# Gate table of an expert layer: GpSimd builds the gated one-hots alone, and 22 expert units are multiplied in split form

## The chip, the core and the metric

The kernel runs on one core of a Trainium2 chip. Its engines are called as the profile calls them: PE (TensorE, the matrix engine; PEld is its weight load), DVE (VectorE), ACT (ScalarE), POOL (GpSimd), and SP, whose queue starts the DMAs. The metric is the device time of one launch in microseconds. Before the change it is 2589.73 us, the median of 3 runs (2589.39 to 2591.72).

## The reference

Two layers of a transformer-like block and then a second block of another kind; the change touches the feed-forward part of each of the two layers, a "PEER" layer with 16384 experts, of which every token picks 16 for each of 8 heads. Everything is float32.

```python
q = (ht @ w_q).reshape(n_tok, PEER_HEADS, PEER_QDIM)       # 256 tokens, 8 heads
v1, i1 = lax.top_k(s1, PEER_TOPK)                          # 16 best of 128 first keys
v2, i2 = lax.top_k(s2, PEER_TOPK)                          # 16 best of 128 second keys
cand = (v1[..., :, None] + v2[..., None, :])...            # 256 pairs
top, pos = lax.top_k(cand, PEER_TOPK)                      # the 16 best pairs
eidx = jnp.take_along_axis(cidx, pos, axis=-1)             # expert = i1 * 128 + i2
gate = jax.nn.softmax(top, axis=-1)
act = jax.nn.gelu(jnp.einsum('td,thkd->thk', hc, expert_u[ec]), approximate=False)
y = jnp.einsum('thk,thkd->td', gc * act, expert_v[ec])
```

The kernel doesn't gather experts. It computes the product of every token with all 16384 rows of `expert_u`, applies gelu, multiplies by a dense table of gates G (token x 128 x 128, zero where an expert wasn't picked), and multiplies with all of `expert_v`.

## The kernel before

Expert weights come in units of 128 experts x 1024 (0.5 MB) through a ring of 8 slots in SBUF. One unit is 8 products (KD = 8) of a 128x128 piece of weights with a 128x256 piece of activations. There are two ways to multiply it. In *plain* form float32 goes straight to PE. In *split* form ACT first copies the unit rounded to the reduced type fp32r (the high part), DVE subtracts that from the unit (the low part, written in the unit's own ring slot), and PE makes three fp32r products for each piece: high x high, high x low, low x high.

The block that matters here chooses the routes. In its first part PE computes the queries and DVE finds the top 16 of everything. PE meanwhile works ahead: 22 pairs of expert units (AHEAD = 22, 44 units), whose gelu is spilled to DRAM and fetched back in the next block. `ahead()` (L1088 on) is a generator that yields after each of the 8 products of a unit, so that other work can be laid between them. 11 pairs (AHEAD_PICK) are done while DVE picks.

Then comes the gate table. For each of the 16 x 8 = 128 routes of a token (on the partitions, after three transposes of PICK) J holds the first index, the second index and the gate. G of one token is a 128x128 matrix: the product over the 128 routes of the one-hot of the first index with the one-hot of the second index times the gate. A group is four tokens, and there are GROUPS = 64. For a group

- DVE (L1270) makes both one-hots with one comparison of iota with the indices, 128x1024;
- POOL (L1209) multiplies the second half by the gates, in place, 128x512;
- PE (L1128) does four float32 products of 128x128 into one PSUM bank, and then as many products of the units ahead as `ahead_by` says (some 2.6 for each group);
- ACT (L1192) copies the bank into G.

The one-hots have HOTS = 3 buffers, so DVE may start group g when PE has multiplied group g - 3. They lie where the high parts of the ring lie otherwise. In this block all the units ahead are in plain form; the activations H32 lie in WK, the tile `work`. The order on each engine is written out by hand, and engines wait for each other by counting semaphores (`wait_ge`). At the end ACT and DVE split the first three units of the next block (L345, L350), and the block ends for all engines together.

Of the kernel before, what the change touches and what calls it, by code (L numbers as in the profile page):

```python
# [22 lines left out]
ALU = mybir.AluOpType  # L23
# [7 lines left out]
P = 128  # L31
# [120 lines left out]
def program(nc, wstream, consts, mixconst, crow, xT, memT, pos, vec2, s5b, s5c, wglu, wdt, out):  # L152
    ctx = ExitStack()
    with ctx:
# [451 lines left out]
        for layer in range(DEPTH):  # L606
# [433 lines left out]
            def ahead_by(g):  # L1040

                return KD + KD * (2 * (AHEAD - AHEAD_PICK) - 1) * (g + 1) // GROUPS

            with nc.Block() as block:
# [23 lines left out]
                def _(pe):  # L1068
# [24 lines left out]
                    def ahead():  # L1093

                        for p in range(AHEAD):
                            if p >= 2:
                                pe.wait_ge(S("ahead_gelu"), p - 1)
                            for e in range(2):
                                u = S_EXP + 2 * p + e
                                arrived(pe, u)  # L1100
                                if p + e == 0:
                                    pe.wait_ge(S("h_whole"), KD)
                                for k in range(KD):
                                    mm = pe.matmul(PS[:, 6 + p % 2, e * T:(e + 1) * T],  # L1104
                                                   RING[:, u % SLOTS, k * P:(k + 1) * P], H32[:, k, :],
                                                   start=(k == 0), stop=(k == KD - 1))
                                    if k == KD - 1:
                                        mm.then_inc(units_used, 1)
                                    yield

                    first = ahead()
                    for _ in range(2 * KD * AHEAD_PICK):
                        next(first)
# [7 lines left out]
                    for _ in range(KD):  # L1121
                        next(first)
                    for g in range(GROUPS):
                        pe.wait_ge(S("gated"), g + 1)
                        if g >= 4:
# [4 lines left out]
                        mm.then_inc(S("g_made"), 1)  # L1130
                        for _ in range(ahead_by(g) - (ahead_by(g - 1) if g else KD)):
                            next(first)
# [4 lines left out]
                def _(sc):  # L1137
# [43 lines left out]
                    by_tile(0, SEL[:, 0, :])  # L1181
                    for p in range(9, AHEAD_PICK):
                        ahead_gelu(p)
                    by_tile(1, SEL[:, 1, :])
                    by_tile(2, GT.rearrange("p a b -> p (a b)"))
                    for i in range(3):
                        act.wait("routes_turned", i + 1)
                        act.mark(sc.activation(J[:, i, :], PS[:, nxt(), 0:T], ACT.Copy), "bank_emptied")
                    p = AHEAD_PICK
                    for g in range(GROUPS):  # L1190
# [3 lines left out]
                        if ahead_by(g) >= 2 * KD * (p + 1 - AHEAD_PICK):  # L1194
                            ahead_gelu(p)
                            p += 1
                        if g >= GROUPS - PRE:
                            split_high(act, S_EXP + V0 + g - (GROUPS - PRE), True)
# [7 lines left out]
                def _(pool):  # L1206
                    for g in range(GROUPS):
                        pool.wait_ge(S("one_hots"), g + 1)
                        pool.tensor_tensor(hots[g % HOTS][:, 1], hots[g % HOTS][:, 1],  # L1209
                                           J[:, 2, 4 * g:4 * g + 4].unsqueeze(2).to_broadcast([P, 4, P]),  # L1210
                                           ALU.mult).then_inc(S("gated"), 1)

                @block.vector
                def _(dve):
# [52 lines left out]
                    for g in range(GROUPS):  # L1267
                        if g >= HOTS:
                            v.wait("g_made", g - HOTS + 1)
                        v.mark(dve.tensor_tensor(hots[g % HOTS], J[:, 0:2, 4 * g:4 * g + 4].unsqueeze(3)  # L1270
                                                 .to_broadcast([P, 2, 4, P]),
                                                 iota.unsqueeze(1).unsqueeze(1).to_broadcast([P, 2, 4, P]),
                                                 ALU.is_equal), "one_hots")
                    highs = N_WQ - PRE
                    for q in range(PRE):
# [1208 lines left out]
```

## Time and profile before

| | us |
|---|---|
| median of 3 runs | 2589.73 |
| the profiled execution | 2592.32 |
| its span, first to last instruction | 2590.5 |
| PE busy | 2423.0 (94%) |
| DVE busy | 1764.7 (68%) |
| ACT busy | 1092.7 (42%) |
| POOL busy | 237.5 (9%) |
| POOL L1209, all 128 | 228.0 |

The profiled execution has 1.8 us around its span, and is 2.6 us above the median of the runs. The gate table is built twice, once for each layer, between about 308 and 442 us and between about 1301 and 1435 us. A float32 product of PE has two records in the trace, an fp32r product one. Records of PE overlap, so what one costs is the distance from start to start, not the duration of one. A record of POOL or DVE that waits for a shared resource is longer by the wait.

### The profile page before, as it was taken

What the parts mean: (1) busy time and instruction counts of PE and PEld (TensorE: products, weight loads), DVE (VectorE), ACT (ScalarE), POOL (GpSimd) and SP (SyncE); (2) the same over time, 40 slices, a digit from 0 to 9 for tenths busy, and PEclk for the clock granted to TensorE, in tenths of its full rate; (3) what the DMA queues carried; (4) which work ended last, traced back from release to release, by engine and by line L of the source; (5) the groups of instructions that cost most, each with busy time, mean ns of one, the idle gap of its engine ahead of it and who ended that gap; (6) DMA issues with size and microseconds to landing.
All of it is one profiled execution on the core that took longest, in us unless ns stands there. A gap on an engine that the chain in (4) does not pass through costs nothing. (4 is left out here: it accounts for less than half of the span.)

```text
span 2590.5 us, 38298 instructions
## 1 busy us (share of the span) xinstructions
PE 2423.0 (94%) x15240; PEld 2218.0 (86%) x15240; DVE 1764.7 (68%) x2789; ACT 1092.7 (42%) x1592; POOL 237.5 (9%) x141
## 2 busy tenths in 40 slices
PE   4789999999999999979999999999999987798998
PEld 4679898889999999879889789999999876787998
DVE  7969966676666666668977675555555577545665
ACT  4442233444444444444133444444444332343554
POOL 0000286000000000000088000000000000000000
PEclk9889999999999999989999999999999989898999
DMA  8354533786666666424633585555555421351553
GB/s 343 118 200 160 173 106 114 248 310 237 229 236 236 236 230 207 135 82 139 187 114 114 195 313 189 187 186 186 186 186 187 161 90 57 114 163 66 191 188 110
DMA packets 133037, 460.58 MB, mean 178 GB/s; under 512 B 15152, under 2 KB 15408, under 8 KB 132400
## 3 DMA queue, kind: packets, MB, share of 16 engines
q1 hardware_dynamic: 132912, 458.90, 52.3%
q8 instruction: 80, 1.31, 0.2%
q14 instruction: 45, 0.37, 0.0%
HBM read 445.73 MB, written 13.11 MB: 177 GB/s over the span
## 5 line engine op out<-in xcount | busy, mean ns | idle before, releaser
L1451 DVE TENSOR_TENSOR ring_lo<-ring,ring_hi 128x1024 fp32r<-128x1024 f32 x421 | 515.0, 1225 | 310.6 <-ACT ring_hi L1385 310.6
L1385 ACT ACTIVATE ring_hi<-ring 128x1024 fp32r<-128x1024 f32 x421 | 445.1, 1057 | 396.2 <-PE banks L335 242.4
L308 PE MATMUL banks<-normed_hi,ring_hi 128*128 128x256 f32 x2096 | 598.8, 286 | 8.5 <-DVE ring_lo L350 8.5
L310 PE MATMUL banks<-normed_hi,ring_lo 128*128 128x256 f32 x2096 | 594.3, 284 | 0.0
L309 PE MATMUL banks<-normed_lo,ring_hi 128*128 128x256 f32 x2096 | 594.2, 284 | 0.0
L308 PEld LDWEIGHTS banks<-normed_hi,ring_hi 128*128 128x128 f32 x2096 | 403.1, 192 | 13.8 <-ACT arena L2148 8.7
L333 PE MATMUL banks<-ring_hi,work_lo 128*128 128x512 f32 x1024 | 402.1, 393 | 11.0 <-DVE work_lo L1472 11.0
L309 PEld LDWEIGHTS banks<-normed_lo,ring_hi 128*128 128x128 f32 x2096 | 403.1, 192 | 3.8
L310 PEld LDWEIGHTS banks<-normed_hi,ring_lo 128*128 128x128 f32 x2096 | 403.0, 192 | 0.0
L334 PE MATMUL banks<-ring_lo,work_lo 128*128 128x512 f32 x1024 | 401.4, 392 | 0.0
L335 PE MATMUL banks<-ring_hi,work_lo 128*128 128x512 f32 x1024 | 400.4, 391 | 0.0
L1104 PE MATMUL banks<-work,ring 128*128 128x256 f32 x1408 | 325.8, 379 | 0.0
L350 DVE TENSOR_TENSOR ring_lo<-ring,ring_hi 128x1024 fp32r<-128x1024 f32 x185 | 224.0, 1222 | 108.3 <-ACT ring_hi L345 107.9
L1104 PEld LDWEIGHTS banks<-work,ring 128*128 128x128 f32 x1408 | 257.5, 190 | 29.5
L1209 POOL TENSOR_TENSOR one_hots<-one_hots,routes 128x512 f32<-128x512 f32 x128 | 228.0, 1811 | 546.9 <-DVE one_hots L1270 546.9
L333 PEld LDWEIGHTS banks<-ring_hi,work_lo 128*128 128x128 f32 x1024 | 193.9, 189 | 50.0 <-DVE work_lo L1472 11.8
L1270 DVE TENSOR_TENSOR one_hots<-routes,consts_sb 128x1024 f32<-128x1024 f32 x128 | 185.4, 1465 | 73.4 <-PE banks L1128 69.4
L345 ACT ACTIVATE ring_hi<-ring 128x1024 fp32r<-128x1024 f32 x185 | 194.5, 1055 | 89.2 <-PE banks L310 67.7
L335 PEld LDWEIGHTS banks<-ring_hi,work_lo 128*128 128x128 f32 x1024 | 193.4, 189 | 41.1
L334 PEld LDWEIGHTS banks<-ring_lo,work_lo 128*128 128x128 f32 x1024 | 194.0, 189 | 37.2
L1192 ACT ACTIVATE arena<-banks 128x512 f32<-128x512 f32 x128 | 76.4, 597 | 169.7 <-PE banks L1128 169.7
L1128 PEld LDWEIGHTS banks<-one_hots 128*128 128x128 f32 x1024 | 134.0, 192 | 8.9 <-POOL one_hots L1209 2.3
(345 smaller groups left out, 3030.5 us busy)
## 6 DMA issues: line engine op xcount, KB each, us to landing
ring<-wstream SPq DMA_DIRECT2D x716, 512.0 KB, 3.3
arena<-wstream SPq DMA_DIRECT2D x96, 512.0 KB, 5.3
spill<-one_hots SPq DMA_DIRECT2D x44, 256.0 KB, 4.2
rstd<-spill SPq DMA_DIRECT2D x16, 256.0 KB, 3.9
pool_and_keys<-spill SPq DMA_DIRECT2D x14, 256.0 KB, 3.9
routes<-spill SPq DMA_DIRECT2D x14, 256.0 KB, 3.7
residual<-xT SPq DMA_DIRECT2D x1, 1024.0 KB, 9.1
arena<-mixconst SPq DMA_DIRECT2D x2, 512.0 KB, 4.8
```

The lines of the kernel that those rows point to most:

```text
L308: pe.matmul(dst, w_hi[:, o], hi[:, k, :], start=(k == 0), stop=False)
L309: pe.matmul(dst, w_hi[:, o], lo[:, k, :], start=False, stop=False)
L310: mm = pe.matmul(dst, w_lo[:, o], hi[:, k, :], start=False, stop=(k == KD - 1))
L333: pe.matmul(dst, hi[:, t], w_hi[:, o], start=first, stop=False)
L334: pe.matmul(dst, hi[:, t], w_lo[:, o], start=False, stop=False)
L335: mm = pe.matmul(dst, lo[:, t], w_hi[:, o], start=False, stop=last)
L345: act.mark(act.eng.activation(RING_HI[:, u % HIGHS, :], RING[:, u % SLOTS, :], ACT.Copy), "high")
L350: v.mark(v.eng.tensor_tensor(RING_LO[:, u % SLOTS, :], RING[:, u % SLOTS, :], RING_HI[:, u % HIGHS, :].bitcast(F32), ALU.subtract), "split")
L1104: mm = pe.matmul(PS[:, 6 + p % 2, e * T:(e + 1) * T], RING[:, u % SLOTS, k * P:(k + 1) * P], H32[:, k, :], start=(k == 0), stop=(k == KD - 1))
L1209: pool.tensor_tensor(hots[g % HOTS][:, 1], hots[g % HOTS][:, 1], J[:, 2, 4 * g:4 * g + 4].unsqueeze(2).to_broadcast([P, 4, P]), ALU.mult). ...
L1385: sc.activation(RING_HI[:, u % HIGHS, :], RING[:, u % SLOTS, :], ACT.Copy)\
L1451: dve.tensor_tensor(RING_LO[:, u % SLOTS, :], RING[:, u % SLOTS, :], RING_HI[:, u % HIGHS, :].bitcast(F32), ALU.subtract).then_inc(S("spli ...
```

## The change

For each layer:

- POOL no longer waits for DVE. It makes the gated one-hot of the second index by itself: for each of the four tokens of a group one `tensor_scalar` of 128x128 (is iota equal to the index, times the gate), with index and gate as pointer scalars from J. 256 such instructions take the place of 64.
- DVE makes the one-hot of the first index alone (128x512, not 128x1024), and between the groups the low parts of 22 units.
- ACT makes the high parts of these 22 units, in two buffers in WK_LO, which lie over H32. So they can't start before the last plain unit is multiplied.
- PE multiplies these 22 units in split form, 24 fp32r products each. They all stand in the gate loop now; before, one of them stood ahead of it. What stands between the last transpose and the first group is the last of the 22 plain units, held back by one unit.
- ACT does the gelu of the last plain pair after the copies into J, not before them.

```diff
             def ahead_by(g):
-                return KD + KD * (2 * (AHEAD - AHEAD_PICK) - 1) * (g + 1) // GROUPS
+                return max(2 * KD * (AHEAD - AHEAD_PICK) * (g - 1) // (GROUPS - 2), 0)
+            def finished(g):
+                return [n for n in range(2 * (AHEAD - AHEAD_PICK)) if g >= 0 and ahead_by(g - 1) < KD * (n + 1) <= ahead_by(g)]
...
+                                if u >= E0:
+                                    pe.wait_ge(S("split"), S0 + u - E0 + 1)
                                 for k in range(KD):
...
+                                        pe.matmul(dst, WK_LO[:, u % 2, o], H_HI[:, k, :], start=(k == 0), stop=False)
+                                        pe.matmul(dst, WK_LO[:, u % 2, o], H_LO[:, k, :], start=False, stop=False)
+                                        mm = pe.matmul(dst, RING_LO[:, u % SLOTS, o], H_HI[:, k, :],
+                                                       start=False, stop=(k == KD - 1))
...
-                    for _ in range(2 * KD * AHEAD_PICK):
+                    for _ in range(2 * KD * AHEAD_PICK - KD):
                         next(first)
...
                     for g in range(GROUPS):
+                        pe.wait_ge(S("one_hots"), g + 1)
                         pe.wait_ge(S("gated"), g + 1)
...
-                    for p in range(9, AHEAD_PICK):
+                    for p in range(9, AHEAD_PICK - 1):
                         ahead_gelu(p)
...
+                    ahead_gelu(AHEAD_PICK - 1)
+                    def early_high(n):
+                        u = E0 + n
+                        arrived(sc, u)
+                        sc.wait_ge(units_used, u - 1 if n >= 2 else E0)
+                        act.mark(sc.activation(WK_LO[:, u % 2, :], RING[:, u % SLOTS, :], ACT.Copy), "high")
+                    early_high(0)
+                    early_high(1)
...
+                        for n in finished(g):
+                            if n + 2 < N_SPLIT:
+                                early_high(n + 2)
...
                     for g in range(GROUPS):
-                        pool.wait_ge(S("one_hots"), g + 1)
-                        pool.tensor_tensor(hots[g % HOTS][:, 1], hots[g % HOTS][:, 1],
-                                           J[:, 2, 4 * g:4 * g + 4].unsqueeze(2).to_broadcast([P, 4, P]),
-                                           ALU.mult).then_inc(S("gated"), 1)
+                        if g == 0:
+                            pool.wait_ge(S("bank_emptied"), 3)
+                        if g >= HOTS:
+                            pool.wait_ge(S("g_made"), g - HOTS + 1)
+                        for t in range(4):
+                            i = pool.tensor_scalar(hots[g % HOTS][:, 1, t, :], iota, J[:, 1, 4 * g + t:4 * g + t + 1],
+                                                   J[:, 2, 4 * g + t:4 * g + t + 1], ALU.is_equal, ALU.mult)
+                        i.then_inc(S("gated"), 1)
...
-                        v.mark(dve.tensor_tensor(hots[g % HOTS], J[:, 0:2, 4 * g:4 * g + 4].unsqueeze(3)
...
+                        v.mark(dve.tensor_tensor(hots[g % HOTS][:, 0], J[:, 0, 4 * g:4 * g + 4].unsqueeze(2)
+                                                 .to_broadcast([P, 4, P]),
+                                                 iota.unsqueeze(1).to_broadcast([P, 4, P]), ALU.is_equal), "one_hots")
+                        for n in [0] * (g == 2) + [1] * (g == 3) + [n + 2 for n in finished(g - 3)]:
+                            if n < N_SPLIT:
+                                u = E0 + n
+                                v.wait("high", S0 + n + 1)
+                                v.mark(dve.tensor_tensor(RING_LO[:, u % SLOTS, :], RING[:, u % SLOTS, :],
+                                                         WK_LO[:, u % 2, :].bitcast(F32), ALU.subtract), "split")
```

PE, from the last transposes (`consts_sb,arena`) into the first groups of the gate loop (`one_hots`) of layer 0, before. `work,ring` are products of plain units.

```order
L1118 MATMUL banks<-consts_sb,arena 128x128 [waits stage0_9]
L1118 MATMUL banks<-consts_sb,arena 128x128
L1104 MATMUL banks<-work,ring 128x256 [waits loaded4,stage0_0]
L1104 MATMUL banks<-work,ring 128x256 x7
L1128 MATMUL banks<-one_hots 128x128 [waits stage0_11]
L1128 MATMUL banks<-one_hots 128x128 x3
L1104 MATMUL banks<-work,ring 128x256 [waits loaded5]
L1104 MATMUL banks<-work,ring 128x256
L1128 MATMUL banks<-one_hots 128x128 [waits stage0_11]
```

The same place after the change, where `work_lo` holds the high part of a split unit and `ring_lo` its low part:

```order
L1117 MATMUL banks<-work,ring 128x256 [waits loaded3]
L1117 MATMUL banks<-work,ring 128x256 x7
L1146 MATMUL banks<-one_hots 128x128 [waits stage0_12,stage0_11]
L1146 MATMUL banks<-one_hots 128x128 x3
L1146 MATMUL banks<-one_hots 128x128 [waits stage0_12,stage0_11]
L1146 MATMUL banks<-one_hots 128x128 x3
L1146 MATMUL banks<-one_hots 128x128 [waits stage0_12,stage0_11]
L1146 MATMUL banks<-one_hots 128x128 x3
L1120 MATMUL banks<-normed_hi,work_lo 128x256 [waits stage0_5,loaded4,stage0_0]
L1121 MATMUL banks<-normed_lo,work_lo 128x256
L1122 MATMUL banks<-normed_hi,ring_lo 128x256
```

The unit between transposes and first group comes from slot 3, not 4: it is the 22nd, not the 23rd. Three groups stand without a unit's product between them, and each group waits for two engines' one-hots.

DVE, from the end of the routing into the gate loop, the difference (`-` before, `+` after):

```order
-L1270 TENSOR_TENSOR one_hots<-routes,consts_sb 128x1024 [waits stage0_20,stage0_19]
-L1270 TENSOR_TENSOR one_hots<-routes,consts_sb 128x1024 x2
-L1270 TENSOR_TENSOR one_hots<-routes,consts_sb 128x1024 [waits stage0_12] x61
+L1306 TENSOR_TENSOR one_hots<-routes,consts_sb 128x512 [waits stage0_21,stage0_20]
+L1306 TENSOR_TENSOR one_hots<-routes,consts_sb 128x512 x2
+L1313 TENSOR_TENSOR ring_lo<-ring,work_lo 128x1024 [waits stage0_17]
+L1306 TENSOR_TENSOR one_hots<-routes,consts_sb 128x512 [waits stage0_13]
+L1313 TENSOR_TENSOR ring_lo<-ring,work_lo 128x1024 [waits stage0_17]
```

Its comparisons are half as wide, and a subtraction of a whole unit stands behind about every third of them.

POOL, its whole work in the block of layer 0, the difference (of the 64 groups after, the first four are shown):

```order
-L1209 TENSOR_TENSOR one_hots<-one_hots,routes 128x512 [waits stage0_21] x64
+L1245 TENSOR_SCALAR one_hots<-consts_sb,routes 128x128 [waits stage0_21]
+L1245 TENSOR_SCALAR one_hots<-consts_sb,routes 128x128 x11
+L1245 TENSOR_SCALAR one_hots<-consts_sb,routes 128x128 [waits stage0_13]
+L1245 TENSOR_SCALAR one_hots<-consts_sb,routes 128x128 x3
```

Three groups go without a wait, since they have the three buffers; from then on the first instruction of a group waits until PE has multiplied the group three before (stage0_13).

## Rows read from the trace of the kernel before

**Rows 1.** The page, part 1: busy time of PE, share of the span.
```profile
PE 2423.0 (94%) x15240; PEld 2218.0 (86%) x15240; DVE 1764.7 (68%) x2789; ACT 1092.7 (42%) x1592; POOL 237.5 (9%) x141
```

**Rows 2.** Busy time by stretch, the gate loops of both layers; columns as in the second line.
```profile
core 0: us, PE busy (x) PEld busy (x) DVE busy (x) ACT busy (x) POOL busy (x), PEclk, DMA share, GB/s
...
311.00:437.00 126.00, 125.62 (x821) 116.76 (x821) 89.90 (x62) 42.43 (x72) 112.08 (x64) 1.00 0.35 110
...
1304.00:1430.00 126.00, 125.62 (x821) 116.72 (x820) 89.97 (x62) 42.36 (x72) 112.08 (x64) 1.00 0.36 110
```

**Rows 3.** Timeline of PE around the loop's start: start, us, engine, line, records.
```profile
305.80 0.38 PE L1118 MATMUL banks<-consts_sb,arena 128*128 128x128 f32 x2
...
307.53 3.62 PE L1104 MATMUL banks<-work,ring 128*128 128x256 f32 x16
311.53 1.16 PE L1128 MATMUL banks<-one_hots 128*128 128x128 f32 x8 [0.38 <-POOL one_hots L1209]
```

**Rows 4.** Timeline of PE inside the loop.
```profile
338.16 1.05 PE L1128 MATMUL banks<-one_hots 128*128 128x128 f32 x8
339.05 1.03 PE L1104 MATMUL banks<-work,ring 128*128 128x256 f32 x4
```

**Rows 5.** Waits from 311 to 441 us: us in total, times, longest.
```profile
DVE one_hots L1270 <- PE banks L1128: 34.7, 49, 1.0
...
PE banks L1128 <- POOL one_hots L1209: 0.4, 1, 0.4
```

**Rows 6.** Timeline of PE in the queries' products, which are in split form.
```profile
191.23 0.28 PE L308 MATMUL banks<-normed_hi,ring_hi 128*128 128x256 f32 x1
...
192.31 0.28 PE L308 MATMUL banks<-normed_hi,ring_hi 128*128 128x256 f32 x1
```

**Rows 7.** Timeline of DVE and ACT at the end of the routing.
```profile
300.59 4.42 DVE L1260 TENSOR_REDUCE arena<-arena 128x256 f32<-128x4096 f32 x1
...
305.79 0.42 DVE L1264 TENSOR_TENSOR arena<-arena 128x256 f32<-128x256 f32 x1
...
306.00 0.60 ACT L1167 ACTIVATE one_hots<-banks 128x512 f32<-128x512 f32 x1 [6.31 <-PE banks L1104]
...
306.49 0.71 ACT L1171 ACTIVATE arena<-arena 128x256 f32<-128x256 f32 x2
...
307.10 1.01 ACT L1188 ACTIVATE routes<-banks 128x256 f32<-128x256 f32 x3
```

**Rows 8.** Timeline of PE at the end of the loop and after it.
```profile
440.27 1.46 PE L1104 MATMUL banks<-work,ring 128*128 128x256 f32 x6
447.23 0.79 PE L333 MATMUL banks<-ring_hi,work_lo 128*128 128x512 f32 x1 [5.51 <-DVE work_lo L1472]
...
452.09 0.63 PE L335 MATMUL banks<-ring_hi,work_lo 128*128 128x512 f32 x1
...
453.80 0.39 PE L335 MATMUL banks<-ring_hi,work_lo 128*128 128x512 f32 x1
```

**Rows 9.** POOL's multiplication: durations (ns min/median/max), then two overlapping instructions in the timeline.
```profile
L1209 POOL TENSOR_TENSOR one_hots<-one_hots,routes x64: 1032/2016/2059, 309.5 to 436.4; 128x512 f32<-128x512 f32 x64
```
```profile
309.52 1.95 POOL L1209 TENSOR_TENSOR one_hots<-one_hots,routes 128x512 f32<-128x512 f32 x1 [267.82 <-DVE one_hots L1270]
```
```profile
310.49 2.06 DVE L1270 TENSOR_TENSOR one_hots<-routes,consts_sb 128x1024 f32<-128x1024 f32 x1
```

**Rows 10.** Timeline of POOL: its memsets.
```profile
0.24 0.10 POOL L2477 MEMSET const-float32-0.0<- 128x1 f32 x1 [0.24 <-issue]
0.27 0.10 POOL L2477 MEMSET const-float32-1.0<- 128x1 f32 x1
...
40.22 0.52 POOL L658 MEMSET arena<- 128x512 f32 x1 [39.78 <-POOLq L509]
40.68 0.53 POOL L659 MEMSET arena<- 128x516 f32 x1
```

**Rows 11.** Groups of instructions by line and shape: busy us, mean ns | idle before.
```profile
L350 DVE TENSOR_TENSOR ring_lo<-ring,ring_hi 128x1024 fp32r<-128x1024 f32 x185 | 224.0, 1222 | 108.3 <-ACT ring_hi L345 107.9
...
L1460 DVE TENSOR_TENSOR work<-rstd,arena 128x512 f32<-128x512 f32 x16 | 10.9, 684 | 1.1 <-DVE ring_lo L350 1.1
```
```profile
L345 ACT ACTIVATE ring_hi<-ring 128x1024 fp32r<-128x1024 f32 x185 | 194.5, 1055 | 89.2 <-PE banks L310 67.7 <-PE banks L2105 14.5 <-DMA ring<-wstream 6.3
```

More of the change, by code:

```diff
@@ L1040, in ahead_by @@
             def ahead_by(g):
-                return KD + KD * (2 * (AHEAD - AHEAD_PICK) - 1) * (g + 1) // GROUPS
+                return max(2 * KD * (AHEAD - AHEAD_PICK) * (g - 1) // (GROUPS - 2), 0)
+            def finished(g):
+                return [n for n in range(2 * (AHEAD - AHEAD_PICK)) if g >= 0 and ahead_by(g - 1) < KD * (n + 1) <= ahead_by(g)]
+            E0 = S_EXP + 2 * AHEAD_PICK
+            N_SPLIT = 2 * (AHEAD - AHEAD_PICK)
+            S0 = N_WQ - PRE
             with nc.Block() as block:
@@ L1102, in ahead @@
                                     pe.wait_ge(S("h_whole"), KD)
+                                dst = PS[:, 6 + p % 2, e * T:(e + 1) * T]
+                                if u >= E0:
+                                    pe.wait_ge(S("split"), S0 + u - E0 + 1)
                                 for k in range(KD):
-                                    mm = pe.matmul(PS[:, 6 + p % 2, e * T:(e + 1) * T],
-                                                   RING[:, u % SLOTS, k * P:(k + 1) * P], H32[:, k, :],
-                                                   start=(k == 0), stop=(k == KD - 1))
+                                    o = slice(k * P, (k + 1) * P)
+                                    if u < E0:
+                                        mm = pe.matmul(dst, RING[:, u % SLOTS, o], H32[:, k, :],
+                                                       start=(k == 0), stop=(k == KD - 1))
+                                    else:
+                                        pe.matmul(dst, WK_LO[:, u % 2, o], H_HI[:, k, :], start=(k == 0), stop=False)
+                                        pe.matmul(dst, WK_LO[:, u % 2, o], H_LO[:, k, :], start=False, stop=False)
+                                        mm = pe.matmul(dst, RING_LO[:, u % SLOTS, o], H_HI[:, k, :],
+                                                       start=False, stop=(k == KD - 1))
                                     if k == KD - 1:
@@ L1130, in _ @@
                         mm.then_inc(S("g_made"), 1)
-                        for _ in range(ahead_by(g) - (ahead_by(g - 1) if g else KD)):
+                        for _ in range(ahead_by(g) - (ahead_by(g - 1) if g else 0)):
                             next(first)
@@ L1269, in _ @@
                             v.wait("g_made", g - HOTS + 1)
-                        v.mark(dve.tensor_tensor(hots[g % HOTS], J[:, 0:2, 4 * g:4 * g + 4].unsqueeze(3)
[L1271 to L1274, printed above, removed]
+                        v.mark(dve.tensor_tensor(hots[g % HOTS][:, 0], J[:, 0, 4 * g:4 * g + 4].unsqueeze(2)
[7 more added lines that the diff above has]
+                                                         WK_LO[:, u % 2, :].bitcast(F32), ALU.subtract), "split")
+                    assert v.n["split"] == S0 + N_SPLIT
+                    highs = S0 + N_SPLIT
                     for q in range(PRE):
```

## The prediction

> **What bounds the kernel now.** I read the page first: PE is busy 94% of the span [rows 1], so a change is worth what it takes from PE, as long as nobody else becomes late. Then busy time by stretch over the two gate loops: in 126 us PE is busy 125.62, POOL 112.08 and DVE 89.90, at the full granted clock, and the second layer repeats the first to 0.1 us [rows 2]. I work out one layer and double it. Third, the waits: in the loop PE waited 0.4 us for POOL in all, at its first group, while DVE waited 34.7 us for PE to free buffers [rows 5]. So PE sets the pace, but POOL has only about a tenth in hand. Last the timelines, for prices. The reader is to see in them that PE runs without gaps from 311.53 [rows 3] to 440.27 + 1.46 = 441.73 us [rows 8].
>
> **PE's own work.** A plain unit is 16 records, 3.62 us from first start to last end; less the 0.38 of the last, 15 steps: 0.216 each, 3.46 for a unit [rows 3]. In split form nine steps take 192.31 - 191.23 = 1.08 us, 0.12 each [rows 6], so 24 products are 2.88 us. A group's gate products take 339.05 - 338.16 = 0.89 us [rows 4], 57.0 for 64. Before, the loop holds 57.0 and 21 plain units, 72.6: 129.6, which agrees with 441.7 - 311.5 = 130.2. After, it holds 57.0 and 22 split units, 63.4: 120.4. That is -9.2 us. It isn't 22 x 0.58 = 12.7, because one plain unit that was hidden under DVE's routing no longer is: PE now reaches the transposes one unit early, at 305.80 - 3.46 = 302.3 [rows 3], and must wait for the routing.
>
> **The start of the loop.** DVE gives the second index at 305.01 and the normed gates at 306.21. ACT reorders the last two only from 306.49 on, because it does a gelu from 306.00 to 306.60 first; the pair ends at 307.20 [rows 7]. The change takes this gelu away from there, so the last reordering can start at 306.2 and end at 306.6, 0.6 us earlier, and all behind it moves with it: the copies into J end at 307.5 instead of 308.1, and PE's held-back plain unit runs from 306.9 to 310.4. PE's first group stood at 311.53, with 0.38 of wait for POOL [rows 3]; it can stand at 310.4: -1.1 us.
>
> **The first split.** The high parts lie over H32 and can't begin before that plain unit is done. From 310.4: 0.2 to signal, 0.6 for the displaced gelu, 1.06 for the high part, 1.22 for the low part [rows 7, 11] is 313.5. PE has done its three bare groups by 310.4 + 2.7 = 313.1. I take a wait of 0.5 us (0 to 1.5, if POOL holds DVE up). Later splits have slack: a high part starts when its buffer comes free and takes about 1.06 + 1.22 = 2.3 us, while PE multiplies the other unit for 8 / 2.75 = 2.9 groups, some 5.5 us. DVE's load falls from 1.22 a group to 0.68 + 22/64 x 1.22 = 1.10 [rows 11], ACT's rises by 22/64 x 1.06 = 0.36 to about 1.1. Both lie under PE's 1.88 (120.4/64) and cost nothing. Weights come no faster than before they are used, and the loop moves 110 GB/s [rows 2]: nothing there.
>
> **The clock.** The new hole on PE, from 302.3 to about 305.5 and again to 306.6, has a price. The trace shows such a hole: after 5.5 us of idleness wide products take 0.63 us a record until 452.5 and 0.39 later [rows 8], the lower granted level (1.2 GHz) for 5.3 us of work, of which half is lost, 2.6 us. The new hole is shorter and has two transposes in it. Between 0 and 2.6 us for a layer; I take 1.5. Nothing hides it, except where POOL is later than PE anyway.
>
> **POOL.** This decides. No row shows a `tensor_scalar` there. The parts: for a group four instructions of 128x128, and the time that DVE keeps POOL out. That there is such a time is in the rows: a multiplication of 128x512 takes 1.03 us at best and 2.02 in the median, and two that overlap, one on POOL and one on DVE with two operands in SBUF, are each lengthened by about the other [rows 9]. DVE's time with data is (1222 - 684)/512 = 1.05 ns an element [rows 11]: 0.54 for a comparison and 1.08 for a subtraction, 0.54 + 22/64 x 1.08 = 0.91 us a group (before: 1.08, and 1.08 + 0.95 = 2.03 is the whole pace of the loop before, so POOL was nearly a second bound). For one small instruction: from below a memset, which reads nothing, 0.46/512 an element and 0.03 from start to start of tiny ones [rows 10], 0.115 + 0.03 = 0.15 us. From above the multiplication, which reads two tensors, 1.03/512 x 128 = 0.26 with the 0.10 that even a one-column memset lasts added in full [rows 9, 10], 0.36 us. The new one reads one tensor; it is near neither, and I take the middle, 0.255. Then POOL needs 4 x 0.255 + 0.91 = 1.93 us a group. It starts at 307.6 and is done at 307.6 + 64 x 1.93 = 431.1. PE is done at 310.4 + 120.4 + 0.5 = 431.3, plus the clock. A dead heat; for two chains coupled by three buffers I add 1 us.
>
> The Trainium skill, GPSIMD Engine Reference, section "4.1 Engine selection", says that two-input operations are about 2x slower on GpSimd than on VectorE but one-input ones run at roughly line rate; by that, an instruction would be 0.11 us and its dispatch, and POOL would have slack. The same page, "7. Performance pitfalls for Q7 kernels", speaks against the change: it gives about 102 cycles for each small read command, which don't overlap; with a tensor and two pointer scalars that would be an estimate of 0.26 us on top of 0.11, 0.37. No run here shows either.
>
> **Sum for a layer.** -9.2 (PE's work) - 1.1 (start) + 0.5 (first split) + 1.5 (clock) + 1.0 (coupling) = -7.3 us. Twice is -14.6: 2592.3 - 14.6 = 2577.7 for an execution like the profiled one, which is 2.6 above the median, so 2575 us for the median. Between its bounds (no clock loss, no coupling: -9.8 for a layer, 2570; all losses at their most: -4.2, 2581) is the forecast's own range.
>
> **Rivals.**
> 1. *POOL becomes the bound, and the kernel slower.* At 0.36 us an instruction POOL needs 1.44 + 0.91 = 2.35 a group and is done at 307.6 + 150.4 = 458.0, 16.3 later than 441.7 before; twice, 2622 us. It decides from (441.7 - 307.6)/64 = 2.095 a group on, 0.296 us an instruction. For it: four instructions instead of one, each with a start of its own and two pointer scalars to fetch, and DVE's blocking stays. Against: the multiplication's 1.03 us for two tensors leaves little room for a long start. Pointer scalars have no row; at 0.45 it would be 2668. The skill's 0.37 from above would come out here.
> 2. *POOL and PE trade places without gain.* At 0.28 to 0.31 us an instruction POOL ends within 3 us of 441.7 or so: 2584 to 2596.
> 3. *POOL's small pieces let DVE in without loss*, since what an instruction spends ahead of its data overlaps DVE's turn, and the clock doesn't fall: PE alone bounds, 2570. For it: the pace 2.03 before is the sum of the data times alone, with nothing for starts.
> 4. *The splits don't keep up*: a high part behind ACT's copies and a low part behind a blocked DVE come later than 5.5 us. At 1 us for each of 22 units the layer gains nothing: 2590. Against: 3 us of slack each.
>
> **How the numbers follow.** Forecast and rival 3 together 0.57 (0.42 and 0.15), rival 1 0.30, rival 2 0.10, rival 4 0.03. Less than 0.2% (5 us, what can just be told from no change) are most of rival 2 and rival 4. So faster 0.57, same 0.11, slower 0.32. The range begins at 2567, a little under rival 3, and must reach into rival 1: to 2625, its price at 0.36 us, which leaves out 0.15 above (pointer scalars dearer than every row) and some 0.03 below.
>
> **What would show it.** Right: in the loop PE busy over 97%, its rows on the one-hots with waits under 3 us in total; POOL's instructions 0.25 us or less from start to start; last product of layer 0 at 431 to 435 us; after 302 us a hole on PE and some rows of the plain unit at twice their length. Rival 1: hundreds of PE waits for L1245, POOL without idleness, the loop's end past 442. Rival 4: PE waits for L1313. The forecast is wrong if a small POOL instruction costs over 0.29 us.

## The result and the profile after

| | before | after |
|---|---|---|
| median | 2590.72 us (4 runs) | 2809.24 us (4 runs) |
| ratio, 95% interval | | 1.0844 (1.0825 to 1.0863) |
| span of the profiled execution | 2590.5 us | 2808.0 us |
| POOL busy in both gate loops | 228.0 us | 480.0 us |

A fourth run of the kernel before moved its median from 2589.73 to 2590.72. The kernel is 218 us slower, 109 for each layer. It was forecast at 2575 us, some 15 us faster than before, and the time lies far outside the range (2567 to 2625 us). What follows is read as [rows 1] and [rows 2] were. First the page of the changed kernel, part 1, then its costliest POOL group (line, shapes, count | busy us, mean ns | idle before):

```profile
PE 2462.8 (88%) x15592; PEld 2254.0 (80%) x15592; DVE 1722.8 (61%) x2833; ACT 1137.1 (40%) x1636; POOL 489.4 (17%) x525
...
L1245 POOL TENSOR_SCALAR one_hots<-consts_sb,routes 128x128 f32<-128x128 f32 x512 | 480.0, 952 | 514.4 <-ACT routes L1206 514.4
```

Then busy time by stretch in the first gate loop, which now reaches to 551 us:

```profile
311.00:547.00 236.00, 149.97 (x1030) 138.54 (x1028) 72.23 (x85) 67.19 (x98) 236.00 (x253) 0.91 0.21 64
```

POOL is busy for all of the 236 us; PE, which filled its loop before [rows 2], is busy for 64% of it at a mean granted clock of 0.91. POOL's 512 instructions stand in two rows without a pause, 240 us for each layer: 240.0/64 = 3.75 us a group, where PE needs 1.88 by the prediction (1.91 measured further down, in the hybrid with the held-back unit). The first one starts at 307.27, so the last ends at 547.3, and PE's last product is 3.9 us behind that. Before, the loop's last product ended at 441.7 [rows 8]: 551.2 - 441.7 = 109.5 for a layer, 219 for both, which is the whole difference.

A stretch in the middle of the changed kernel's loop, in the timeline (start, us). The three fences show PE, then POOL (the last three instructions of one group, the first three of the next), then DVE:

```profile
405.08 1.13 PE L1146 MATMUL banks<-one_hots 128*128 128x128 f32 x8 [1.21 <-issue]
```
```profile
402.34 0.79 POOL L1245 TENSOR_SCALAR one_hots<-consts_sb,routes 128x128 f32<-128x128 f32 x1
...
403.11 1.09 POOL L1245 TENSOR_SCALAR one_hots<-consts_sb,routes 128x128 f32<-128x128 f32 x1
...
404.19 0.79 POOL L1245 TENSOR_SCALAR one_hots<-consts_sb,routes 128x128 f32<-128x128 f32 x1
...
404.96 0.79 POOL L1245 TENSOR_SCALAR one_hots<-consts_sb,routes 128x128 f32<-128x128 f32 x1
...
405.74 1.93 POOL L1245 TENSOR_SCALAR one_hots<-consts_sb,routes 128x128 f32<-128x128 f32 x1
...
407.65 0.79 POOL L1245 TENSOR_SCALAR one_hots<-consts_sb,routes 128x128 f32<-128x128 f32 x1
```
```profile
402.84 0.69 DVE L1306 TENSOR_TENSOR one_hots<-routes,consts_sb 128x512 f32<-128x512 f32 x1 [2.71 <-PE banks L1146]
405.12 1.36 DVE L1313 TENSOR_TENSOR ring_lo<-ring,work_lo 128x1024 fp32r<-128x1024 f32 x1 [1.59 <-ACT work_lo L1214]
406.40 0.68 DVE L1306 TENSOR_TENSOR one_hots<-routes,consts_sb 128x512 f32<-128x512 f32 x1
```

The reader is to see three things. A small POOL instruction takes 404.96 - 404.19 = 0.77 us from start to start where DVE is quiet; the prediction had 0.255, and its upper bound was 0.36. The instruction that meets DVE's comparison is 0.30 longer (1.09); the one at 405.74 meets what is left of a subtraction and, right behind it, the comparison of 406.40, and is 1.14 longer (1.93) for both. What each costs in the mean comes from a run below, in which the subtractions are missing: 440.1/128 - 3.10 = 0.33 us for a comparison, and (480.0 - 440.1)/44 = 0.91 for a subtraction. 4 x 0.776 + 0.33 + 22/64 x 0.91 is 3.75, as measured. And PE waits 1.2 us before its group, until 0.10 us after the end of the group's last POOL instruction (404.19 + 0.79 = 404.98). The profile calls most of these waits "issue", so the waits for L1245 that the prediction named can't be counted in this view, and POOL's row without pauses shows the bound instead.

### The profile page after: what moved, and what is told of

Same layout as the page of the kernel before. It is cut to its first block and busy times, and to the rows that moved or that the text cites. A ratio compares the mean times of both kernels' runs of the same rounds, so it can differ in the third digit from the quotient of the medians.

```text
span 2808.0 us, 39548 instructions
## 1 busy us (share of the span) xinstructions
PE 2462.8 (88%) x15592; PEld 2254.0 (80%) x15592; DVE 1722.8 (61%) x2833; ACT 1137.1 (40%) x1636; POOL 489.4 (17%) x525
## 5 line engine op out<-in xcount | busy, mean ns | idle before, releaser
L1245 POOL TENSOR_SCALAR one_hots<-consts_sb,routes 128x128 f32<-128x128 f32 x512 | 480.0, 952 | 514.4 <-ACT routes L1206 514.4
L1146 PE MATMUL banks<-one_hots 128*128 128x128 f32 x1024 | 161.7, 306 | 173.5 <-issue 160.0
L1146 PEld LDWEIGHTS banks<-one_hots 128*128 128x128 f32 x1024 | 140.5, 213 | 195.8 <-issue 192.3
L1306 DVE TENSOR_TENSOR one_hots<-routes,consts_sb 128x512 f32<-128x512 f32 x128 | 89.4, 701 | 250.7 <-PE banks L1146 246.7
L1117 PE MATMUL banks<-work,ring 128*128 128x256 f32 x704 | 157.9, 388 | 0.0
```

Of the source, the lines that this page charges most:

```text
L1146: mm = pe.matmul(PS[:, g % 4, t * P:(t + 1) * P], hots[g % HOTS][:, 0, t, :], hots[g % HOTS][:, 1, t, :], start=True, stop=True)
L1245: i = pool.tensor_scalar(hots[g % HOTS][:, 1, t, :], iota, J[:, 1, 4 * g + t:4 * g + t + 1], J[:, 2, 4 * g + t:4 * g + t + 1], ALU.is_equa ...
```

## The experiments

Every ratio below is against runs of the kernel before that were made beside it (medians 2590.98 to 2591.39 us).

### Short series on GpSimd alone

A kernel of its own, in place of the whole program, with eight instructions of each form:

```diff
+                for _ in range(N):
+                    pool.tensor_scalar(new("pool", 128), iota, ia, ga, ALU.is_equal, ALU.mult)
...
+                for _ in range(N):
+                    pool.tensor_scalar(new("pool", 128), iota, 3.0, 2.0, ALU.is_equal, ALU.mult)
...
+                for _ in range(N):
+                    pool.tensor_scalar(new("pool", 512), iota4, ia, ga, ALU.is_equal, ALU.mult)
```

> Leaves out the whole computation: after the loads it runs short series of single instructions, first on GpSimd alone, then on VectorE alone, then on ScalarE alone, then on GpSimd and VectorE together; every instruction has its own output columns. Read is the time from start to start within a series. In the changed kernel a 128x128 tensor_scalar (is_equal, mult, two pointer scalars) stands 0.776 us from the next where VectorE is quiet. Theory A (a fixed price for each instruction): about 0.65 us at 8 columns, 0.71 at 64, 0.78 at 128, under 1.3 at 512. Theory B (a price for each element, 6 ns, because a comparison is slow there): 0.05 to 0.15 us at 8 columns, 0.39 at 64, 0.78 at 128, 3.1 at 512, and clearly less for a multiplication alone. Theory C (the two pointer scalars cost it): the series with immediates runs in under 0.4 us. The 128x512 tensor_tensor should again be 1.03. VectorE's tensor_scalar of 128x128: 0.15 to 0.25 us, from its rows at 64 and 256 columns.

Measured, in the timeline of POOL (the start of one series to the start of the next, over 8, is the price of one; L193 to L201 at 128 columns: both steps with pointers, comparison with pointer, multiplication with pointer, both steps with constants, multiplication with constant; L203 to L209 the full form at 8, 64, 256 and 512 columns):

```profile
10.33 6.22 POOL L193 TENSOR_SCALAR pool_out<-consts_sb,routes 128x128 f32<-128x128 f32 x8 [9.90 <-DMA dve_wide<-xT]
16.52 4.67 POOL L195 TENSOR_SCALAR pool_out<-consts_sb,routes 128x128 f32<-128x128 f32 x8
21.14 4.69 POOL L197 TENSOR_SCALAR pool_out<-consts_sb,routes 128x128 f32<-128x128 f32 x8
25.77 4.93 POOL L199 TENSOR_SCALAR pool_out<-consts_sb 128x128 f32<-128x128 f32 x8
30.64 4.03 POOL L201 TENSOR_SCALAR pool_out<-consts_sb 128x128 f32<-128x128 f32 x8
34.63 3.13 POOL L203 TENSOR_SCALAR pool_out<-consts_sb,routes 128x8 f32<-128x8 f32 x8
37.69 4.53 POOL L205 TENSOR_SCALAR pool_out<-consts_sb,routes 128x64 f32<-128x64 f32 x8
42.14 9.70 POOL L207 TENSOR_SCALAR pool_out<-consts_sb,routes 128x256 f32<-128x256 f32 x8
51.74 16.54 POOL L209 TENSOR_SCALAR pool_out<-consts_sb,routes 128x512 f32<-128x512 f32 x8
68.15 3.43 POOL L211 TENSOR_TENSOR pool_out<-consts_sb,routes 128x128 f32<-128x128 f32 x8
71.44 7.12 POOL L213 TENSOR_TENSOR pool_out<-consts_sb,routes 128x512 f32<-128x512 f32 x7
```

The full form: 0.77 us at 128 columns, 1.20 at 256 (9.60/8), 2.05 at 512. From 256 to 512 columns that is 3.3 ns a column, and some 0.35 us are left at zero columns. So theories A and B each hold half, and C has a small part: the two pointer scalars cost 6.19/8 - 4.87/8 = 0.165 us, 0.08 each. The multiplication of two tensors is cheaper: 0.41 us at 128 columns and 1.0 at 512. At 512 both operands are read with repeats, as the gate is in the kernel, so these two don't give a price for a column; the next run has it for ordinary tensors. On DVE (from the same run, eight in 81.73 - 79.67 us) the full form took 0.26 us at 128 columns, a third of POOL's.

### What in the form is slow

> Leaves out the whole computation, like the first run of short series: GpSimd alone, four of each form, at 128 and at 512 columns. It asks what the changed kernel's instruction pays for. From the first series: 0.494 us for one multiplication by a constant at 128 columns, 0.606 with a comparison in front of it, 0.084 to 0.085 for each pointer scalar, and 3.3 ns a column for the full form. Theory (the price for a column comes with the number of steps: each step is paid apart): a multiplication alone about half the 3.3 ns, so 1.0 to 1.2 us at 512 columns, and multiply and add with constants like compare and multiply, 1.9. Rival (the comparison is the slow part): multiply and add 1.1 us at 512 columns, a comparison alone 1.8. Rival (tensor_scalar costs 3.3 ns a column whatever it does): all forms 1.75 to 2.05 us at 512.

Measured, four of each form, POOL's timeline. L199 and L205 are at 128 columns: multiply and add with constants; copy (L201 is multiply and add with pointers). L207 to L219 are at 512 columns: multiply; compare; compare and multiply; multiply and add, all with constants; multiply and add with pointers; compare with pointer; copy. L221 and L223 are the multiplication of two ordinary tensors.

```profile
16.66 1.08 POOL L199 TENSOR_SCALAR pool_out<-consts_sb 128x128 f32<-128x128 f32 x4
17.73 1.73 POOL L201 TENSOR_SCALAR pool_out<-consts_sb,routes 128x128 f32<-128x128 f32 x4
...
21.72 0.99 POOL L205 COPY pool_out<-consts_sb 128x128 f32<-128x128 f32 x4
22.68 5.86 POOL L207 TENSOR_SCALAR pool_out<-consts_sb 128x512 f32<-128x512 f32 x4
28.51 5.85 POOL L209 TENSOR_SCALAR pool_out<-consts_sb 128x512 f32<-128x512 f32 x4
34.33 7.58 POOL L211 TENSOR_SCALAR pool_out<-consts_sb 128x512 f32<-128x512 f32 x4
41.88 2.36 POOL L213 TENSOR_SCALAR pool_out<-consts_sb 128x512 f32<-128x512 f32 x4
44.23 3.01 POOL L215 TENSOR_SCALAR pool_out<-consts_sb,routes 128x512 f32<-128x512 f32 x4
47.23 6.17 POOL L217 TENSOR_SCALAR pool_out<-consts_sb,routes 128x512 f32<-128x512 f32 x4
53.34 2.27 POOL L219 COPY pool_out<-consts_sb 128x512 f32<-128x512 f32 x4
55.58 0.69 POOL L221 TENSOR_TENSOR pool_out<-consts_sb,routes 128x8 f32<-128x8 f32 x4
56.22 1.15 POOL L223 TENSOR_TENSOR pool_out<-consts_sb,routes 128x64 f32<-128x64 f32 x4
```

All three theories fall. A multiplication alone costs 1.46 us (5.83/4), and so does a comparison alone; both together 1.89; but multiply and add, also two steps, only 0.59, and 0.75 with pointers. So neither the comparison nor the number of steps is what costs. Of the two pairs of steps measured, one runs about three times faster than the other, and as fast as a copy (2.24/4 = 0.56 us); a one-hot can't be made with that pair. Why it is fast no run here shows. The multiplication of two ordinary tensors takes 0.16 us at 8 columns (0.64/4) and 0.41 at 128 (first series), 2.1 ns a column.

The Trainium skill, GPSIMD Engine Reference, section "4.1 Engine selection", calls one-input operations there roughly line rate. Of the forms measured only multiply and add and the copy could be called that, with (2.35 - 1.07)/4 us for 384 more columns, 0.83 ns a column (VectorE's subtraction takes 1.05 [rows 11]); the form of the change takes 3.3 ns, four times as much, and here the measurement decides. The Trainium skill, same page, section "7. Performance pitfalls for Q7 kernels", gives about 102 cycles for each small read command, an estimate of 0.085 us at that page's 1.2 GHz. The 0.08 us of each pointer scalar agrees with it, if a pointer scalar is such a read, which no run here shows.

### The change by halves

**GpSimd's one-hots alone**, all units plain again:

```diff
-                                if u >= E0:
-                                    pe.wait_ge(S("split"), S0 + u - E0 + 1)
...
-                                    if u < E0:
+                                    if True:
...
-                    early_high(0)
-                    early_high(1)
...
-                    highs = S0 + N_SPLIT
+                    highs = S0
```

> The changed kernel with the 22 units of each layer in plain form again, all else as changed. Theory (GpSimd bounds the loop): a group takes 4 x 0.776 plus 0.30 for VectorE's comparison in between, 3.40 us, the loop 218 us; it would end at 525 instead of 547 of the changed kernel, so 2809 - 2 x 22 = 2765 us (2750 to 2780). Rival (the splits cause a good part of the loss, by blocking GpSimd's port or by coming late): 2700 or below. A second rival, that the plain units matter to TensorE, would show TensorE busy over 90% of the loop; expected 60%.

Measured: 2770.75 us, ratio 1.0687 (1.0669 to 1.0705). POOL's 512 instructions took 440.1 us, 3.44 a group for the 3.40 expected; PE was busy 151.3 of 218 us, 69% where 60% was expected. 180 of the 218 us are this half; the other 38 come with the split units, whose 44 subtractions take POOL 0.91 us each.

**The split units alone**, one-hots as before (VectorE compares both, GpSimd multiplies):

```diff
-                        for t in range(4):
-                            i = pool.tensor_scalar(hots[g % HOTS][:, 1, t, :], iota, ...
+                        pool.wait_ge(S("one_hots"), g + 1)
+                        pool.tensor_tensor(hots[g % HOTS][:, 1], hots[g % HOTS][:, 1], ...
```

> The changed kernel with the one-hots made as before (VectorE compares both, GpSimd multiplies by the gates, 128x512), the 22 units in split form. Theory (VectorE and GpSimd exclude each other while they move data): 1.08 + 22/64 x 1.08 + 0.95 = 2.40 us for a group, the loop ends at 307.6 + 154 + 2 = 463 instead of 442, 21 for a layer, 2633 us (2620 to 2645). Rival (only TensorE's work counts, the two overlap in part): 2575 to 2585, as forecast for the changed kernel.

Measured: 2632.33 us, ratio 1.0162 (1.0145 to 1.0178), against 2633 from the theory. This half alone is slower too. The groups of DVE from 307 to 425 us, and after them one of POOL's over the whole kernel:

```profile
L1302 DVE TENSOR_TENSOR one_hots<-routes,consts_sb 128x1024 f32<-128x1024 f32 x51 | 85.8, 1728 | 2.3 <-ACT routes L1206 1.7 <-PE banks L1146 0.6
L1310 DVE TENSOR_TENSOR ring_lo<-ring,work_lo 128x1024 fp32r<-128x1024 f32 x17 | 32.5, 1909 | 3.6 <-ACT work_lo L1214 3.6
```
```profile
L1241 POOL TENSOR_TENSOR one_hots<-one_hots,routes 128x512 f32<-128x512 f32 x128 | 250.4, 1980 | 571.7 <-DVE one_hots L1302 571.7
```

DVE is idle for only 5.9 of these 118 us, and its instructions last 1.73 and 1.91 us, where the subtraction takes 1.22 elsewhere [rows 11] and the comparison 1.21 at its shortest in the kernel before. The rest fits POOL's turns: DVE's and POOL's times with data, as the expectation estimated them, add up to 2.40 us a group, and the loop took 151.2 us from PE's first group to its last product, 2.36 a group. So the change needed something like its other half: the splits have no room beside the old one-hots.

### One wide instruction

```diff
-                        for t in range(4):
-                            i = pool.tensor_scalar(hots[g % HOTS][:, 1, t, :], iota, J[:, 1, 4 * g + t:...
+                        pool.tensor_scalar(hots[g % HOTS][:, 1], iota.unsqueeze(1).to_broadcast([P, 4, P]),
+                                           J[:, 1, 4 * g:4 * g + 1], J[:, 2, 4 * g:4 * g + 1],
```

> The changed kernel, but GpSimd makes one tensor_scalar of 128x512 for a group, with the index and the gate of the first of the four tokens for all four: three of four tokens get wrong gates. As many elements as the changed kernel, a quarter of the instructions. Theory A (fixed price for each instruction): 0.8 to 1.2 us for the one instruction plus 0.4 to 0.9 of VectorE's turns, under TensorE's 1.88, so the loop is TensorE's: 2570 to 2580 us. Theory B (price for each element): 3.1 us an instruction, 2800 or more.

Measured: 2633.74 us, ratio 1.0166 (1.0149 to 1.0183). Neither expectation was right: they were made for a price wholly fixed or wholly for elements. POOL's instruction lasted 2.44 us in the mean, 310.3 us for 128, 2.42 a group: the 2.05 of the short series and 0.37 of DVE's turns. Even without three of the four starts GpSimd would still bound the loop.

### GpSimd out of the loop

VectorE makes the gated one-hots too, GpSimd's part is left out, and PE waits for `one_hots` alone:

```diff
+                        dve.tensor_tensor(hots[g % HOTS][:, 0], J[:, 0, 4 * g:4 * g + 4]...
+                        for t in range(0, 4):
+                            i = dve.tensor_scalar(hots[g % HOTS][:, 1, t, :], iota, J[:, 1, 4 * g + t:4 * g + t + 1],
+                                                  J[:, 2, 4 * g + t:4 * g + t + 1], ALU.is_equal, ALU.mult)
+                        v.mark(i, "one_hots")
```

With plain units, in the kernel before:

> The kernel before, all units plain, but VectorE makes the gated one-hots too (one tensor_tensor of 128x512 for the first index, four tensor_scalars of 128x128 for the second) and GpSimd does nothing. By the short series VectorE needs 0.602 + 4 x 0.256 = 1.63 us for a group. Theory (before, TensorE alone set the pace of 2.03 us; GpSimd at 1.03 + 1.0 of blocked time was a second bound just under it): no change, 2588 to 2591. Rival (the blocking between VectorE and GpSimd cost something before): 2580 or below.

Measured: 2588.7 us, ratio 0.9989 (0.998 to 0.9998). PE was busy 114.00 of 114 us, and its loop took 129.9 us where it took 130.2 before. Before the change, GpSimd wasn't what held the loop.

With split units, in the changed kernel:

> The changed kernel with GpSimd's work given to VectorE, as in the run before it. VectorE: 0.602 + 4 x 0.256 + 22/64 x 1.137 = 2.02 us for a group, TensorE 1.88. Theory (the slower of the two bounds the loop, nothing else): VectorE bounds, the loop ends at 307.3 + 129 + 1 = 438 instead of 442, 4 for a layer: 2583 us (2578 to 2590). Rival (blocking, not GpSimd's own pace, was what cost): TensorE bounds, 2573. If the splits themselves come late: over 2600.

Measured: 2589.21 us, ratio 0.999 (0.9981 to 0.9999). DVE was busy 111.77 of 114 us, as the theory has it; the time lies in its range, but 6 us above the 2583. 220 us of loss are gone by taking POOL's instructions away, with the splits kept.

Without the held-back unit:

```diff
-                    for _ in range(2 * KD * AHEAD_PICK - KD):
+                    for _ in range(2 * KD * AHEAD_PICK):
                         next(first)
...
-                    for _ in range(KD):
-                        next(first)
                     for g in range(GROUPS):
```

> As the run before it, but the last plain unit is not held back: TensorE does all 22 ahead of the transposes and has no hole there. Theory: no half clock at the loop's start, but VectorE bounds the loop from its first one-hot on, so the same time within 2 us for a layer: 2580 to 2584. Rival (the hole and the half clock delay everything behind them): 5 us faster than the run before it.

Measured: 2585.12 us, ratio 0.9972 (0.9961 to 0.9984). Here the rival was right, with 4.1 us. With the unit held back, DVE made the one-hots of three groups and then stood for 2.2 us (311.2 to 313.4 in layer 0), because the subtraction that is next waits for ACT's first high part, and that lies over H32 and waits for the held-back unit, which ran at half clock. Without it DVE goes on without a pause. Twice 2.2 is most of what the run before it missed. The theory's "no half clock" didn't hold: PE stood 2.3 us before its first group, and the granted clock was 0.55 in the 2 us after it (310 to 312).

### A version that is faster than both

GpSimd makes one of the four tokens, VectorE three, split units, nothing held back:

```diff
-                        for t in range(4):
+                        for t in range(1):
                             i = pool.tensor_scalar(hots[g % HOTS][:, 1, t, :], iota, ...
...
+                        for t in range(1, 4):
+                            i = dve.tensor_scalar(hots[g % HOTS][:, 1, t, :], iota, ...
```

> As the run before it, but of the four tokens of a group GpSimd makes the first's gated one-hot (one tensor_scalar of 128x128), VectorE the other three. VectorE 0.602 + 3 x 0.256 + 0.39 = 1.76 us for a group and some blocking, GpSimd 0.774 and up to 0.7 of blocking, TensorE 1.88. Theory: TensorE bounds; first group at about 309, then 120.4 and 1 for the first split, 430.5 instead of 441.7: 11 for a layer, 2568 us (2565 to 2576). Rival (each of VectorE's turns waits behind GpSimd's 0.77): VectorE at 2.1 to 2.4 a group, 2590 to 2630.

Measured: 2570.42 us, ratio 0.9919 (0.9905 to 0.9932). Busy time by stretch in its loop:

```profile
311.00:425.00 114.00, 113.49 (x980) 113.08 (x980) 109.34 (x265) 59.80 (x90) 84.51 (x61) 1.00 0.40 121
```

PE is busy 113.49 of 114 us, DVE 109.34: both nearly full, and PE sets the pace (POOL waited 28.6 us for PE between 307 and 425 us, PE 2.6 for DVE). Its start isn't free either: PE stood 2.1 us before its first group, and three groups then took 4.46 us at a granted clock of 0.50 (308 to 310), where they take 2.84 in the next run. Three more runs take it apart. With the unit held back as in the changed kernel (the diff above the other way round):

> The hybrid (GpSimd one token in four, VectorE three, split units) with the last plain unit held back behind the transposes, as the changed kernel has it. This is the case the forecast priced: TensorE bounds the loop, with the hole and the half clock ahead of it. Theory (the forecast's other terms were right and only GpSimd's price was not): 2573 to 2580 us, 3 to 8 more than the hybrid's 2570, since one plain unit is no longer covered (3.46 us) and runs at half clock (2.8 us), against what the hybrid itself loses by waiting for its first one-hots. Rival (the hold is free, since TensorE waits for the one-hots anyway): within 1 us of the hybrid.

Measured: 2578.35 us, ratio 0.9953 (0.9939 to 0.9967), 8 more than the hybrid. PE's timeline at the loop's start in this run, and below it the held-back unit of the second layer:

```profile
301.08 0.38 PE L1135 MATMUL banks<-consts_sb,arena 128*128 128x128 f32 x2
304.27 0.44 PE L1135 MATMUL banks<-consts_sb,arena 128*128 128x128 f32 x2 [2.81 <-ACT arena L1189]
305.47 0.69 PE L1135 MATMUL banks<-consts_sb,arena 128*128 128x128 f32 x2 [0.76 <-ACT arena L1189]
305.95 6.41 PE L1117 MATMUL banks<-work,ring 128*128 128x256 f32 x16
312.20 2.84 PE L1146 MATMUL banks<-one_hots 128*128 128x128 f32 x24
315.34 0.35 PE L1120 MATMUL banks<-normed_hi,work_lo 128*128 128x256 f32 x1 [0.31 <-DVE ring_lo L1318]
```
```profile
1295.79 4.74 PE L1117 MATMUL banks<-work,ring 128*128 128x256 f32 x16
```

The hole of 2.8 us, the plain unit at half clock in 6.41 us instead of 3.62 [rows 3], the bare groups, and 0.31 us of wait for the first split: these are the pieces of the start that were forecast. The half clock costs 2.8 us in the first layer and 1.1 in the second (4.74 - 3.62), where 1.5 for each was taken.

With plain units in the kernel before, to see whose the gain is:

> The kernel before, all units plain, with the hybrid's one-hots (GpSimd one token in four, VectorE three). Theory (the hybrid's gain is all TensorE's, from the split units): 2586 to 2591, as with VectorE doing all. Rival (the one-hots' new division gains by itself): under 2580.

Measured: 2588.61 us, ratio 0.9989 (0.998 to 0.9998). So of the hybrid's 21 us, 18 are the split units' and the start's.

With two tokens on GpSimd (`range(2)` and `range(2, 4)`), to see the bound move:

> The hybrid with two tokens in four on GpSimd. In the hybrid one instruction of 0.774 us lasts 1.41 in the mean, so VectorE's turns take 0.64 us of GpSimd's time for each group. Theory (GpSimd's price and these turns add up, and bound the loop from 1.88 us on): 2 x 0.774 + 0.64 = 2.19 us a group, the loop ends about 20 us later than the hybrid's: 2610 us (2600 to 2620). Rival (GpSimd fills the gaps of VectorE, which has less to do now): 2570 to 2575.

Measured: 2621.05 us, ratio 1.0114 (1.0099 to 1.013). POOL's 256 small instructions a layer are now 128, 291.5 us for both layers, 2.28 a group: 2 x 0.774 and 0.73 of turns, 0.09 more than expected, and the time is 1 us above the range. One token more costs 50 us.

## Why the prediction was wrong, point by point

- **PE bounds before, POOL is nearly a second bound**: right. With POOL idle the time changed by 2.4 us (0.9989), and the time of the split units alone came out of the sum of DVE's and POOL's data times to 1 us.
- **One small POOL instruction**: this is the step that failed. The prediction put it "From above the multiplication, which reads two tensors, 1.03/512 x 128 = 0.26 with the 0.10 that even a one-column memset lasts added in full", took 0.36 as the upper end and chose 0.255. Measured: 0.774. Both parts of the bound were too low. The start cost was taken from a memset, which reads nothing, and is 0.35 us with two pointers, not 0.10; and the price for a column was taken from a multiplication of two tensors as if fewer inputs must be cheaper, and is 3.3 ns, not 1.03/512 = 2.0. The start makes 0.25 of the 0.41 us above the upper end, the columns 0.17. Another operation of the same engine was no bound on this one. The rival mechanism was named rightly, and the point from which it decides (0.296 us) too; its price of 0.36 gave 2622 us. Its own sum with 0.774 would give 4.01 us a group and 2834; with the measured 0.65 for DVE's turns it is 3.75 and 2801, and 3.9 us for each layer, in which PE finishes behind POOL's last instruction and which the rival left out, make it 2809.
- **DVE's turns**, 0.91 us a group: too high for small pieces. In the mean a comparison costs POOL 0.33, not 0.54, and a subtraction 0.91, not 1.08. Together 0.65. That part of POOL's start passes beside DVE's data would explain it, but no run shows that.
- **PE's work, -9.2 us; start -1.1; first split +0.5; clock +1.5; coupling +1.0**, together -7.3 a layer: borne out as a sum where GpSimd is quick enough. The hybrid with the held-back unit has all these terms, and came to -13.0 for both layers, -6.5 a layer. Its loop, from PE's first group to its last product, took 122.2 us instead of 130.2, -8.0 where PE's work, first split and coupling make -7.7. Singly, the clock cost 2.8 us in the first layer, more than its upper bound of 2.6, and 1.1 in the second, 2.0 in the mean for the 1.5 taken; the first split cost less (0.31 and 0.30).
- **Splits keep up**: right. In the changed kernel no wait of PE is put down to L1313, which says little, since PE stood behind POOL there. In the hybrid with the held-back unit, where PE sets the pace, it waited for the low parts once in each layer, 0.31 and 0.30 us, and that is the first split.
- **What would make it wrong**: "if a small POOL instruction costs over 0.29 us". It did, and that was the thing with no row in the trace. The range reached only to the rows' own upper end, and 0.15 was left for dearer pointer scalars; with the deciding price unknown, its upper end had no right to be a sum of two other operations.
- **Slips in the sums**, which decide nothing: the stated upper ends of the losses (2.6 for the clock, 1.5 for the first split, with the 1.0 taken for the coupling) add up to -5.2 us a layer and 2579 us, not -4.2 and 2581. And by rival 2's own terms POOL at 0.28 us would end 4.2 us before 441.7, not within 3.

## What to carry to other kernels

When a change puts a form of instruction on an engine where the trace has no row of it, and a pace hangs on its price, a bound built from other forms of that engine is not a bound; a short series of the very form, 122 us of device time here, would have settled this case. On GpSimd, count starts as well as elements, and price the very form: four instructions of 128 columns cost 3.1 us, one of the same form with 512 columns 2.05, a multiplication of 512 columns 1.0. And where VectorE and GpSimd feed one consumer, the split between them can be tuned: in this kernel a quarter of the pieces on GpSimd filled the gap (0.9919) where half of them (1.0114) and all of them (1.0844) made it the bound.

## What the runs showed of the hardware that was not expected

- GpSimd's `tensor_scalar` of 128x512, float32: 0.59 us for multiply and add, 1.46 for a multiplication or a comparison alone, 1.89 for compare and multiply. Two steps can be faster than one.
- VectorE's turn costs GpSimd more than the other way round when GpSimd's pieces are small: in the hybrid POOL's instruction went from 0.79 to a mean of 1.40 us, DVE's subtraction from 1.22 to 1.23. The first short series ended with both engines at once: 24 of POOL's instructions took 24.2 us instead of 24 x 0.774 = 18.6, while DVE's comparison of 512 columns took 0.62 instead of 0.60.
- A hole of 2.8 us on PE, then a transpose, 0.5 to 0.8 us of nothing and another, was followed by the lower clock level (granted clock 0.50) in both layers of all six kernels that hold the unit back. The unit's 3.62 us became 5.9 to 6.4 in ten of the twelve cases and 4.7 and 4.9 in the other two. Shorter holes, 2.1 us in the hybrid and 2.3 without the held-back unit, were followed by the lower level too (granted clock 0.50 and 0.55 in the next 2 us), which no expectation had.
